# Second MLP product of a two-layer encoder step as seven block products on pairs of units instead of eight

## What is computed

```python
x = x + jnp.concatenate([o_a, o_b, o_c, o_d], axis=-1) @ w_out
x = x + jnp.square(jax.nn.relu(rmsnorm(x, norm_mlp) @ mlp_w1)) @ mlp_w2      # 1024 -> 4096 -> 1024
x = x + (pl @ ple_w_proj) * jax.nn.sigmoid(rmsnorm(x, norm_ple) @ ple_w_gate)
```

## Time and profile before

| | us |
|---|---|
| median of 3 runs (lowest, highest) | 1653.35 (1653.05, 1655.88) |
| the profiled execution, its own time | 1650.54 |
| its span, first to last instruction | 1648.7 |
| PE busy | 1568.4 (95% of the span) |
| PEld busy | 1484.6 (90%) |
| DVE busy | 906.4 (55%) |
| POOL busy | 641.0 (39%) |
| ACT busy | 485.7 (29%) |

### The profile page before, as it was taken

The page is one execution under the profiler, slowest core; times in us unless marked ns, Lnnn a source line. Parts: engine busy times, 40 slices in busy tenths (PEclk is TensorE's granted clock), DMA queues, the critical chain, the costliest instruction groups (busy, mean ns, idle before and its releaser), DMA issues.

```text
span 1648.7 us, 32921 instructions
## 1 busy us (share of the span) xinstructions
PE 1568.4 (95%) x14582; PEld 1484.6 (90%) x14582; DVE 906.4 (55%) x1370; ACT 485.7 (29%) x798; POOL 641.0 (39%) x313
## 2 busy tenths in 40 slices
PE   6999998899999999999899999988999999999995
PEld 6889786699999999999898887767999999999995
DVE  6865576456345371754577555754572635527553
ACT  6521333432111111134345213334311111111332
POOL 3344111164344443465533431203643444434652
PEclk9999999899999999999999999998999999999998
DMA  5211010132222222322222110102222222222221
GB/s 201 69 40 41 27 46 33 34 102 90 90 88 84 86 90 90 91 90 78 84 76 65 41 41 27 52 14 75 87 90 90 89 82 87 90 90 90 90 77 67
DMA packets 43804, 122.61 MB, mean 74 GB/s; under 512 B 10960, under 2 KB 13776, under 8 KB 43536
## 3 DMA queue, kind: packets, MB, share of 16 engines
q1 hardware_dynamic: 43520, 118.74, 23.0%
q10 hardware_dynamic: 144, 1.78, 0.3%
HBM read 116.75 MB, written 3.76 MB: 73 GB/s over the span
## 4 chain that ended last, share of the span: by engine, by line
PE 81%; DVE 11%; ACT 4%; issue 2%; POOL 1%; DMA 0%; SPq 0%; POOLq 0%; DVEq 0%; ACTq 0%
PE psum_p L1342 62%; PE psum_p L1377 6%; PE psum_t L1392 5%; DVE conv_out L960 2%; PE psum_p L1533 1%; PE psum_p L1513 1%; PE psum_p L1362 1%; DVE probs L1158 1%; PE psum_t L1503 1%; PE psum_t L1506 1%; PE psum_p L1385 1%; DVE softmax_columns L1149 1%; DVE mla_q L989 1%; ACT w_high L651 0%; ACT probs L730 0%
## 5 line engine op out<-in xcount | busy, mean ns | idle before, releaser
L1342 PE MATMUL psum_p<-hidden,w_high 128*128 128x272 f32 x5952 | 1000.2, 289 | 13.5 <-DVE misc L941 4.7
L1342 PEld LDWEIGHTS psum_p<-hidden,w_high 128*128 128x128 f32 x5952 | 843.2, 188 | 19.4 <-POOL w_rest L568 7.0
L568 POOL TENSOR_TENSOR w_rest<-raw,w_high 128x1024 fp32r<-128x1024 f32 x210 | 513.9, 2447 | 877.6 <-ACT w_high L651 877.6
L1342 PE MATMUL psum_p<-hidden,w_rest 128*128 128x272 f32 x2976 | 614.9, 287 | 0.0
L1342 PEld LDWEIGHTS psum_p<-hidden,w_rest 128*128 128x128 f32 x2976 | 465.3, 188 | 0.0
L651 ACT ACTIVATE w_high<-raw 128x1024 fp32r<-128x1024 f32 x210 | 222.7, 1060 | 819.7 <-PE psum_p L1342 784.1
L1179 DVE TENSOR_TENSOR x<-psum_p,x 128x544 f32<-128x544 f32 x80 | 58.0, 725 | 281.5 <-PE psum_p L1342 281.5
L929 DVE CAST hidden<-rope 128x544 fp32r<-128x544 f32 x64 | 157.2, 2457 | 2.2
L924 DVE SCALAR_TENSOR_TENSOR hidden<-x,parameters,hidden 128x544 fp32r<-128x544 f32 x48 | 90.7, 1890 | 44.3 <-ACT hidden L668 43.0
L1192 DVE SCALAR_TENSOR_TENSOR rope_in<-psum_p,rms 128x544 f32<-128x544 f32 x64 | 46.4, 725 | 109.2 <-PE psum_p L1342 100.6
L580 POOL TENSOR_TENSOR x_squares_summed<-x_squares_summed,x_squared 128x544 f32<-128x544 f32 x43 | 72.6, 1689 | 53.2 <-ACT x_squared L674 47.2
(11 more groups left out here) (247 smaller groups left out, 1384.1 us busy)
## 6 DMA issues: line engine op xcount, KB each, us to landing
raw<-w_units SPq DMA_DIRECT2D x210, 512.0 KB, 3.5
x<-x_t SPq DMA_DIRECT2D x8, 272.0 KB, 6.4
y_t<-y SPq DMA_DIRECT2D x8, 272.0 KB, 2.1
constants<-consts ACTq DMA_DIRECT2D x1, 1737.5 KB, 8.3
ple_in<-p_t SPq DMA_DIRECT2D x2, 544.0 KB, 4.6
w_kv<-w_kv SPq DMA_DIRECT2D x2, 256.0 KB, 5.1
ckv_p<-mla_c SPq DMA_DIRECT2D x2, 256.0 KB
...
```

The lines of the kernel that those rows point to most:

```text
L568: mark(pool.tensor_tensor(wlo[:, s, :], raw[:, ring(l, u, RAW), :], whi[:, s, :].bitcast(F32), ALU.subtract), lo_done)
L1342: ins = pe.matmul(pp[:, 2 * b + h, 0:HALF], w[:, s, cols(k)], rhs[:, k, part, h * HALF:(h + 1) * HALF], start=(n == 0 and z == 0), stop=(n ...
```

## The change

The second product is done on two by two blocks. Rows of blocks are a pair of output units (x tiles 2p and 2p + 1), the inner index is even or odd hidden tiles, and columns are the two token halves. So a pair is a 2x2 by 2x2 product of blocks, eight block products in the plain way; the change does it with seven, from sums of blocks on both sides (A11, S1, S2, S4, S3, A12, A22 are the names of the weight blocks, in PE's order), and puts the result together from the seven.

- **Weights.** `mlp_w2`'s rows are packed even tiles first. Of a pair of units, three blocks of 512 columns are taken as they are (A11, A12, A22), four are sums: S1 = A21 + A22, S2 = S1 - A11, S4 = A12 - S2, S3 = A11 - A21. DVE makes the sums (`pair_sum`, lines 1461 to 1467, inputs in SBUF). ACT makes all seven high parts (`pair_high`, line 855). POOL makes the rests of A11, S4, S3, A12 and A22 (`pair_rest`, line 753), DVE those of S1 and S2 (`sum_rest`, line 1474).
- **Hidden side.** A pair of hidden tiles now gives seven parts of 272 tokens. DVE makes the squares and four differences (1490 to 1497), ACT the high parts (870, in place of the cast), DVE the rests (1479).
- **Blocks on PE.** `pair_product` (line 1733 issues the matmuls): 4 tile pairs x 3 parts = 12 matmuls of 272 columns into one bank of `psum_t`; four banks in turn.
- **Putting together.** ACT copies A11's result (line 863); DVE does the other six: S1's into two tiles' second halves (1519), S2's and S3's by way of `pair_parts` (1523, 1524, 1526, 1527), three into x directly (1531).
- **Places.** High and rest parts lie in a ring of six half units (three units) instead of two units; raw units have four places in the MLP. A weight block's place is free when PE is through with the block six half units before.
- **Order.** In a pair, DVE does the sums and rests of the next pair between the evacuations. ACT's and POOL's lists are those of the diff.
- The rests of the ple input (L1447) move to DVE in the first product of group 1, with ACT making the high parts; for the norm after the MLP ACT also makes a scaled copy of x in float32, so that DVE's rest there is a plain difference.

```diff
+            def pair_sum(l, g, p, k):
...
+                dve.wait_ge(*proj.at(l, pair_follows(g, p, k) + 1))
+                if k == K_S1:
+                    wait_raw(dve, l, u)
+                    wait_raw(dve, l, u + 1)
+                    ins = dve.tensor_tensor(dst, second[:, 0:512], second[:, 512:D], ALU.add)
...
+                link(dve, ins, sums, l)
...
+            def sum_rest(l, g, p, k):
...
+                dve.wait_ge(*hi_done.at(l, pair_out(g, p, k) + 1))
+                mark(dve.tensor_tensor(wlo_at(s, 1), sum_at(s), f(whi_at(s, 1)), ALU.subtract), lo_sums)
...
             def mlp_group(l, g):
                 for i in range(KT):
-                    o = U_MLP + g * 2 * KT + i
+                    o = mlp_out(g, i)
                     dve.wait_ge(*proj.at(l, o + 1))
 
                     link(dve, dve.scalar_tensor_tensor(two(xr[:]), psum_of(l, o), 0.0, two(rms[:]), ALU.max, ALU.mult),
                          freed, l)
-                    step(dve.tensor_tensor(t1[:], xr[:], xr[:], ALU.mult), l)
-                    split_to(l, lambda z: hb[l][:, i, z, :], t1[:], hidden)
-                for m in range(KT):
-                    add_out(l, U_MLP + g * 2 * KT + KT + m, m)
...
+                    if i % 2 == 0:
+                        step(dve.tensor_tensor(hq[:, 0:8:7, :], two(xr[:]), two(xr[:]), ALU.mult), l)
+                        mark(dve.tensor_tensor(hq[:, 1, :], hq[:, 7, :], hq[:, 0, :], ALU.subtract), h_parts)
+                        hidden_rest(l, g, i // 2, 0, 2)
+                    else:
+                        step(dve.tensor_tensor(hq[:, 2:4, :], two(xr[:]), two(xr[:]), ALU.mult), l)
+                        link(dve, dve.tensor_tensor(hq[:, 4, :], hq[:, 3, :], hq[:, 1, :], ALU.subtract), h_parts, l)
+                        mark(dve.tensor_tensor(hq[:, 5, :], hq[:, 3, :], hq[:, 7, :], ALU.subtract), h_parts)
+                        mark(dve.tensor_tensor(hq[:, 6, :], hq[:, 2, :], hq[:, 4, :], ALU.subtract), h_parts)
+                        hidden_rest(l, g, i // 2, 4, 5)
+                        hidden_rest(l, g, i // 2, 2, 4)
+                        hidden_rest(l, g, i // 2, 5, 7)
+                    if i == KT - 3:
+                        pair_sum(l, g, 0, K_S1)
+                    elif i == KT - 2:
+                        pair_sum(l, g, 0, K_S2)
+                        pair_sum(l, g, 0, K_S4)
+                        sum_rest(l, g, 0, K_S1)
+                        sum_rest(l, g, 0, K_S2)
+                    elif i == KT - 1:
+                        pair_sum(l, g, 0, K_S3)
...
+                        if k == K_S1:
+                            both = x[:, m:m + 2, HALF:TOK]
+                            link(dve, dve.tensor_tensor(both, bank.unsqueeze(1).to_broadcast([P, 2, HALF]), both, ALU.add),
+                                 freed, l)
+                        elif k == K_S2:
+                            dve.wait_ge(*copied.at(l, PAIRS * g + p + 1))
+                            link(dve, dve.tensor_tensor(pq[:, 1, :], bank, pq[:, 0, :], ALU.add), freed, l)
+                            step(dve.tensor_tensor(two(x[:, m, :]), two(x[:, m, :]), pq[:, 0:2, :], ALU.add), l)
...
+                        if p + 1 < PAIRS:
+                            if k == K_S2:
+                                pair_sum(l, g, p + 1, K_S1)
+                            elif k == K_S4:
+                                pair_sum(l, g, p + 1, K_S2)
+                            elif k == K_S3:
+                                pair_sum(l, g, p + 1, K_S4)
+                            elif k == K_A12:
+                                pair_sum(l, g, p + 1, K_S3)
+                                sum_rest(l, g, p + 1, K_S1)
+                            elif k == K_A22:
+                                sum_rest(l, g, p + 1, K_S2)
+                        if g == GROUPS - 1 and p and k in (K_A11, K_S1):
+                            norm_split(l, 2, m - 2 + (k == K_S1))
```

ACT's list after the first product of a group, and POOL's:

```diff
+                    pair_high(l, g, 0, K_S3)
+                    pair_high(l, g, 0, K_A12)
+                    for p in range(PAIRS):
+                        if p:
+                            pair_high(l, g, p, K_A12)
+                        copy_first(l, g, p)
+                        pair_high(l, g, p, K_A22)
+                        if g == GROUPS - 1 and p:
+                            for m in (2 * p - 2, 2 * p - 1):
+                                norm_high(l, 2, m)
+                                square_x(l, 2, m)
+                        if p < PAIRS - 1:
+                            for k in (K_A11, K_S1, K_S2, K_S4, K_S3):
+                                pair_high(l, g, p + 1, k)
...
+                for g in range(GROUPS):
+                    for i in range(0 if g else SPLIT, KT):
+                        rest(l, U_MLP + 2 * KT * g + i)
+                    for p in range(PAIRS):
+                        pair_rest(l, g, p)
+                        if g == GROUPS - 1 and p:
+                            add_square(l, 2, 2 * p - 2)
+                            add_square(l, 2, 2 * p - 1)
```

More of the change, by code:

```diff
@@ L97 @@
+RAW_NTH, RAW_BEFORE = raw_uses()
 class Signal:
@@ L513, in _ @@
                              ).then_inc(loads.sem, 16)
-                for u in range(3, U_OUT + 2 * RAW):
+                for u in range(3, U_OUT + 4):
                     load_unit(l, u)
```

393 lines of the change are left out of this document (306 added, 87 removed).

## The result

The changed kernel takes **1717.01 us** (median of 4 runs, 1708.49 to 1718.71) against 1653.53 in the same comparison: ratio **1.0367**, 95% interval 1.0352 to 1.0382, so slower by 3.7%. The forecast was 1702 (1640 to 1740). The profiled execution took 1716.95 us.

A forecast was written before the change was run, and what follows sets the result against it. PE was taken to set the MLP's time. Added waits of 79 + 3 + 10 + 4 less 48 for removed matmuls gave +48 on 1650.54, so 1699, and 1702 us by the median; range 1640 to 1740.

The forecast's parts named there:

- Meeting (a): In each pair's loop, DVE's rest S1 waits for POOL's rest S4, both reading SBUF: 0.94 us.
- Meeting (b): In each pair's loop, POOL's rest of A11 falls beside DVE's sum S1: another 0.94 us.
- rival A: DVE and POOL meetings miss the path, so pairs run at PE's pace: 1634 us, not slower; chance 16%.
- (1): Lead-in from unit 7's end to the first pair's S3: PE waits 2.7 us per group.
- (2): From a group's first to its second pair: PE waits 3.2 us, and 0.3 behind it.
- (3): A group's two further pairs: 1.83 us longer each, 3.7 per group.
- (5): Each layer's last group, with more DVE rests and POOL sums in a pair: +4.8 us, twice, +10.
- (4): Group 1, with two rests of the ple input on DVE before unit 6: +1.4 us, twice, +3.
- (6): Ple start, where the ple weights' rest on POOL stands behind two longer sums: +2.1 us, twice, +4.
- rival C: Four DVE and POOL meetings a loop, or PE's clock falls in the waits: 1747 us; chance 8%.
- Rival B: One DVE and POOL meeting per loop instead of two, 22 us less: 1680 us; chance 14%.
- D: Blocks' matmuls slower, since 12 in a row accumulate in one bank: +17 us at 5%, 1719 us; chance 2%.

The follow-up runs named there:

- e9: The change with S2's and S3's additions to x taken from PSUM, and later pairs' sums S1 and S2 kept in PSUM and made earlier; 1657.9 us, ratio 1.0011.
- e1: The change with POOL writing zeros in place of its weight rests in the pairs, so five blocks' low parts are left out; 1636.1 us, ratio 0.9889.
- e2: The change with DVE's sums and rests of the second to fourth pair replaced by same-size instructions with one SBUF input; 1670.3 us, ratio 1.0092.
- e3: The change with unused matmuls added on PE before block S1 of the second pair (24) and of the third and fourth (12 each); 1707.1 us, ratio 1.0327.

## Why the prediction was right

**Removed work: right.** 384 matmuls fewer; and a pair of e9 at PE's own pace lasts 10.5 us, as 84 x 0.1254 said.

**Prices: right.** 512 columns on DVE alone 0.69 (estimate 0.69), on ACT 0.63 (0.63), on POOL alone 1.27 to 1.28 (1.25, bounds 1.20 and 1.29).

**The mechanism: right, with one meeting in another place.** Meeting (a), POOL's rest S4 against DVE's rest S1, comes in every pair: all 24 rests of S1 made between pairs take 1.64 to 1.67 us, with 24 waits of PE at L1474, as forecast "once a pair, about 24". Meeting (b) was put at sum S1. There it comes in every group's first pair (1.66 us at 632.21) and in the later pairs of the layers' last groups, but in the other groups' second and third pairs sum S1 takes 0.69. In a third pair POOL meets the addition L1524 just ahead of it instead (1.82 us at 658.49), which costs the loop about the same; in a second pair, where PE has run at the lower clock and POOL is through with its rests by then, L1524 and sum S1 both go free. e1 and e2 show the exclusion from both sides: without the second SBUF input on DVE, or without POOL's reads, the rests take 0.69. So rival A fell. Of the Trainium skill, "SBUF — State Buffer", Who interferes with whom, says that DVE with two SBUF inputs and a GpSimd instruction that reads SBUF contend, and agrees with these traces (1.26 to 1.32 us against 0.69); the note in "Advanced Engine Details and Errata", VectorE Performance Modes, which names only DVE's 2-port modes, doesn't, taken alone.

**The sizes, step by step** (waits of PE, us):

| step | forecast | measured |
|---|---|---|
| (1) lead-in, 8 times | 2.7 each, 21.6 | 1.73 to 1.85, 14.1 |
| (2) first to second pair, 8 times | 3.5 each, 28 | six of 3.6; two of 2.2, where the clock had fallen before; 26.2 |
| (3) third pair, six groups | 1.8 each, 11 | 0.49 to 0.64, 3.6 |
| (3) fourth pair, six groups | 1.8 each, 11 | 1.69 to 1.74, 10.3 |
| (3) and (5), two last groups | 17 | 11.4 |
| (4) group 1, twice | 3 | 1.8 |

Together 67.4 where the steps come to 92. The step that was mis-sized is the third pair of (3). It took PE's pace for given, but after wait (2) PE runs at the lower level and loses 3.3 us, and DVE catches up by that. For (1), the way from unit 7's end to PE's start at S3 was forecast as 8.7 us, 0.7 of it for a late DVE and a meeting, and took 7.9 (622.49 to 630.40). (6) Ple start, forecast +4: the waits for `ple_out` are 7.9 us in all (longest 2.8) against 6.3 before (longest 2.0).

**What the sum lacked: the clock.** It stood in rival C at 8%. It took 28.9 us of PE's pace in the second products, and the waits came 25 us short, two errors against each other, largely of one cause; e3, with the clock nearly held up, shows 100 us of added time there, the change 105.5, the sum 92. So the 1702 near 1717 is earned for the loops and partly luck for the clock. The chance of C was too low, since the earlier trace rows showed the clock around a single wait of 2.0 us only, not after two. C's clock came; four meetings in a loop (L1524, sum S1, sum S2 and rest S1) came only in a group's first pair, where step (2) had three or four, and in some pairs of the last groups.

**Rival B** (one meeting, 1680): only the loops of ordinary second pairs have just one, so B is out. **D** (slower blocks): L1733's matmuls have a mean of 0.298 to 0.309 us against 0.288 to 0.291 of L1689, but in e1, at clock 0.987, 0.287 to 0.293: it was the clock, not the bank. D is out.
